# The pool mixer in another order: rows times weights first, then means less the row as products with a constant band matrix

## What is computed

```python
POOL_WINDOWS = (2, 4, 8, 16)          # one for each group of 256 channels

def pool_mixer(h, w_pool, b_pool, ls):
    ...
    for g, w in enumerate(POOL_WINDOWS):
        xg = hf[..., g * POOL_CH:(g + 1) * POOL_CH]
        cs = jnp.concatenate([jnp.zeros_like(xg[:, :1]), jnp.cumsum(xg, axis=1)], axis=1)
        lo = jnp.clip(t - w // 2, 0, n)
        hi = jnp.clip(t + w // 2, 0, n)
        mean = (cs[:, hi] - cs[:, lo]) / (hi - lo).astype(jnp.float32)[:, None]
        outs.append(mean - xg)
    p = jnp.stack(outs, axis=2).astype(h.dtype)
    y = jnp.einsum('bngc,gcd->bngd', p, w_pool) + b_pool
    return y.reshape(h.shape) * ls

def modulate(x, g, shift, scale):
    return rmsnorm(x, g) * (1.0 + scale) + shift
...
    x = x + g1 * y_lat                              # y_lat = pool_mixer(a_lat, ...), the same for the context
    x = x + g2 * hier_moe(modulate(x, norm2_g[i], sh2, sc2), ...)
```

## Time and profile before

| | before |
|---|---|
| median of 3 runs | 2318.79 us (2317.77 to 2321.14) |
| profiled execution | 2315.83 us, its span 2314.4 us |
| TensorE busy | 2145.6 us (93% of the span) |
| DVE, ACT, POOL busy | 1326.8, 1033.6, 155.3 us |
| granted TensorE clock, mean | 0.963 of full speed |

### The profile page before, as it was taken

How to read it: one execution, slowest core, us unless ns; L and a number is a source line. 1 busy time by engine, 2 the same in 40 slices (tenths; PEclk the granted TensorE clock), 3 DMA queues, 4 the chain that set the end, 5 groups by cost and what they waited for, 6 DMA issues and landing times.

```text
span 2314.4 us, 31372 instructions
## 1 busy us (share of the span) xinstructions
PE 2145.6 (93%) x13228; PEld 1644.9 (71%) x13228; DVE 1326.8 (57%) x1866; ACT 1033.6 (45%) x1499; POOL 155.3 (7%) x128
## 2 busy tenths in 40 slices
PE   4879989999996998999889999998999998999997
PEld 3556655577775675777667888886777776888885
DVE  4767766666637775355536766435254545766633
ACT  3446642155625664387744433324233354433321
POOL 0312200000001220000010000003000002000000
PEclk8989999999997998999999999999999999999998
DMA  9689980022217995211012222222222112322210
GB/s 397 282 317 369 380 346 0 0 110 111 80 48 286 350 359 195 109 37 37 37 73 109 109 75 108 109 91 68 78 88 94 47 40 84 122 83 109 107 58 37
DMA packets 39613, 320.67 MB, mean 139 GB/s; under 512 B 7167, under 2 KB 8191, under 8 KB 20735
## 3 DMA queue, kind: packets, MB, share of 16 engines
q1 hardware_dynamic: 26328, 285.44, 31.9%
q0 software_dynamic: 10624, 25.71, 3.3%
q10 hardware_dynamic: 2512, 7.41, 0.8%
HBM read 306.93 MB, written 24.19 MB: 143 GB/s over the span
## 4 chain that ended last, share of the span: by engine, by line
PE 83%; DVE 7%; ACT 4%; DMA 3%; issue 1%; SPq 1%; POOL 0%; ACTq 0%; POOLq 0%; DVEq 0%
PE PS L163 78%; PE PS L815 2%; PE PS L565 1%; DMA ring<-in_wmod 1%; DVE work L2230 1%; DMA work<-tokens,slots 1%; ACT work L1499 1%; PE PS L1076 1%; DVE WR L2236 1%; DVE work L1741 1%; ACT work L1504 0%; ACT L1504 0%; DMA tokens<-work 0%; ACT work L1495 0%; DVE XH L1728 0%
## 5 line engine op out<-in xcount | busy, mean ns | idle before, releaser
L163 PE MATMUL PS<-HS,RS 128*128 128x512 f32 x4128 | 953.4, 392 | 11.2 <-DVE HS L2007 8.6
L163 PEld LDWEIGHTS PS<-HS,RS 128*128 128x128 f32 x4128 | 775.6, 189 | 177.8 <-issue 14.0
L1685 DVE TENSOR_TENSOR RS<-ring,RS 128x1024 fp32r<-128x1024 f32 x212 | 258.8, 1224 | 344.7 <-ACT RS L1186 344.7
L1186 ACT ACTIVATE RS<-ring 128x1024 fp32r<-128x1024 f32 x212 | 221.4, 1051 | 255.3 <-PE PS L163 255.3
L1596 ACT ACTIVATE work<-work,vec 128x512 f32<-128x512 f32 x88 | 71.8, 816 | 239.8 <-DVE work L2354 239.8
L1685 DVE TENSOR_TENSOR CR<-ring,WR 128x1024 fp32r<-128x1024 f32 x128 | 153.3, 1221 | 39.3 <-ACT WR L1186 36.8
L1186 ACT ACTIVATE WR<-ring 128x1024 fp32r<-128x1024 f32 x128 | 134.8, 1058 | 55.1 <-PE PS L163 46.6
L163 PE MATMUL PS<-work 128*64 128x128 f32 (+5 forms) x1696 | 142.6, 305 | 8.3 <-DVE work L2293 4.4
L1186 ACT ACTIVATE work<-PS 128x384 f32<-128x384 f32 (+2 forms) x194 | 86.8, 484 | 130.0 <-PE PS L1076 45.8
L163 PEld LDWEIGHTS PS<-work 128*64 128x64 f32 (+2 forms) x1696 | 107.7, 148 | 37.9 <-issue 21.3
L163 PE MATMUL PS<-RS,HS 128*128 128x512 f32 x480 | 116.3, 401 | 8.2 <-DVE HS L2007 8.2
(11 more groups left out here) (250 smaller groups left out, 2842.4 us busy)
## 6 DMA issues: line engine op xcount, KB each, us to landing
ring<-in_wexp SPq DMA_DIRECT2D x32, 2048.0 KB, 11.0
ring<-in_wmod SPq DMA_DIRECT2D x24, 2048.0 KB, 10.4
ring<-in_ffnu SPq DMA_DIRECT2D x22, 2048.0 KB, 8.1
ring<-in_wexp SPq DMA_DIRECT2D x32, 1024.0 KB, 11.2
ring<-in_ffnd SPq DMA_DIRECT2D x10, 2048.0 KB, 7.2
ring<-in_dilqk SPq DMA_DIRECT2D x6, 2048.0 KB, 8.1
ring<-in_sbqk SPq DMA_DIRECT2D x4, 2048.0 KB, 8.1
ring<-in_dilv SPq DMA_DIRECT2D x3, 2048.0 KB, 8.1
```

Source lines behind the costliest of these rows:

```text
L163: return T.matmul(out, l, r, start=start, stop=stop, skip_group_check=True)
L1186: return S.activation(out, x, ACT.Copy, **kw)
L1685: V.tensor_tensor(lo, src, hi.bitcast(F32), ALU.subtract).then_inc(w_lo, 1)
```

## The change

The linear map and the mean along the tokens commute, so the order is turned round. First PE multiplies the scaled and shifted rows with the mixer's weights (`z`), tokens on partitions: a tile of 128 tokens is the stationary operand, the weights move, and one `z` is 128 tokens by 512 channels. ACT and DVE copy it out of PSUM in turns. Then `means` multiplies, for each chunk of 128 channels, the tiles of `zt` with a constant band matrix, `band`, which holds mean less row, 144 columns a tile, with two narrow pieces of 8 columns for the ends of a stream. DVE multiplies by the gate and adds to `XL` and `XC` in one instruction; the bias has been added there by POOL before. The sliding sums, their zeros and their patches go, and so does ACT's step behind the products. The constant comes in with the mixer's weights (2688 columns in place of 2048); the table for the stream ends goes (64 columns).

The latent stream is done first, then the context. ada 8, 9 and 10 stand behind the spreads of the second norm, ada 11 inside `route` behind the logits, and the row products of 14 and 15 behind the first three slot products (`info`). Some semaphores are renamed, and three memsets at the start become one.

```diff
         def pool_mix():
-            for n in (4, 5):
-                ada(n, 6 + n % 2)
-            pe.wait_ge(ld_work, 16)
-            pe.wait_ge(md_a, 16)
-            for g in range(4):
-                pe.wait_ge(pw_win, g + 1)
-                for mo in range(2):
-                    for s, (o, L) in enumerate(((0, 512), (512, 256))):
-                        i = 4 * g + 2 * mo + s
-                        pe.wait_ge(pl_y, i - 3)
-                        for k in range(2):
-                            x = mm(PS[:, 2 + i % 4, 0:L], poolw[:, g, k, mo * 128:(mo + 1) * 128],
-                                   PT[:, 2 * g + k, o:o + L], k == 0, k == 1)
-                        x.then_inc(pl_mm, 1)
...
+            def z(i):
+                t, hf = z_of(i)
+                pe.wait_ge(ld_work, 16)
+                free("z", i)
+                for g in (2 * hf, 2 * hf + 1):
+                    pe.wait_ge(md_b, 8 * (t // 4) + 2 * g + 2)
+                    for k in range(2):
+                        x = mm(PS[:, bank["z", i], g % 2 * 256:g % 2 * 256 + 256], HT[:, 2 * g + k, t * 128:(t + 1) * 128],
+                               poolw[:, g, k, :], k == 0, k == 1)
+                x.then_inc(pl_z, 1)
...
+                for j, t in enumerate(tiles):
+                    for q in (n for n in range(12) if z_of(n) == (t, c // 4)):
+                        pe.wait_ge(*z_copied(q))
+                    zc = zt[:, t, c * 128:(c + 1) * 128]
+                    if j == 0:
+                        mm(out[:, 0:8], zc, B[:, 144:152], True, False)
+                    a, b = (16 if j == 0 else 0), (128 if j + 1 == len(tiles) else 144)
+                    x = mm(out[:, 128 * j - 8 + a:128 * j - 8 + b], zc, B[:, a:b], False, False)
+                    if j + 1 == len(tiles):
+                        x = mm(out[:, 128 * j + 120:128 * j + 128], zc, B[:, 152:160], False, True)
+                x.then_inc(pl_mm, 1)
...
+            for i in range(4):
+                z(i)
+            ada_cols(4, 6)
+            for i in range(4, 8):
+                z(i)
+            pe.wait_ge(ad_mod, 4)
+            ada_rows(5, 7)
+            ada_cols(5, 7)
+            for c in range(8):
+                means(c)
+                if c > 2:
+                    stat_add(2, c - 3)
+                if c == 4:
+                    pe.wait_ge(ad_mod, 5)
+                    ada_rows(6, 6)
+            for i in range(8, 12):
+                z(i)
...
+            pe.wait_ge(pl_x, 16)
+            stat_spread(2)
+            stat_spread(3)
+            for n in (8, 9, 10):
                 ada(n, 6 + n % 2)
...
             pe.wait_ge(md_a, MD[1 + 2 * layer] + 8 * len(segs))
+            if layer == 0:
+                ada(11, 7)
...
+            scaled(0, 0, (0,), lambda c, s: HT[:, c, 0:512], 2)
+            for i in (0, 2, 4, 6):
+                z(i)
             ada(4, 6)
             ada(5, 7)
             pool_gates()
...
+            scaled(0, 0, (1,), lambda c, s: HT[:, c, 512:768], 2)
+            for i in range(8):
+                add(i)
+            z(8)
+            z(10)
+            ada(6, 6)
+            for i in range(8, 16):
+                add(i)
...
+        pool.wait_ge(ad_aff, 6)
+        for s, X in enumerate((XL, XC)):
+            pool.wait_ge(md_a, 8 * s + 8)
+            for c in range(8):
+                G.tensor_scalar(X[:, c, :], X[:, c, :], plv[:, 1, c, s:s + 1], None, ALU.add).then_inc(pl_b, 1)
...
-        Y.dma_start(W(12000, 2048), A["poolw"]).then_inc(ld_work, 16)
+        Y.dma_start(W(12000, 2688), A["poolw"]).then_inc(ld_work, 16)
```

More of the change, by code:

```diff
@@ L178, in build @@
     md_a, md_b = sem("mod_scaled"), sem("mod_shifted")
[L179 removed]
+    pl_z, pl_zd, pl_za, pl_mm, pl_b, pl_x = [sem("pool_" + n) for n in (
+        "z", "z_dve", "z_act", "means", "biased", "x")]
     rt_lg, rt_lt, rt_tr, rt_exp, rt_m, rt_rk, rt_blk = [sem("route_" + n) for n in ("logits", "biased", "turned", "exp", "chosen", "rank", "blocks")]
@@ new lines, in means @@
+            def means(i):
+                s, c = i // 8, i % 8
+                tiles = (range(4), range(4, 6))[s]
+                B, out = band[:, c // 2, :], PS[:, bank["b", i], :]
+                free("b", i)
+                for j, t in enumerate(tiles):
[9 more added lines that the diff above has]
+                x.then_inc(pl_mm, 1)
@@ L543, in route @@
                 rank_products()
-            else:
+            for e in range(3):
+                info(layer, nt, e)
+            if layer == 0:
                 pe.wait_ge(th_c, 12)
@@ L1224, in pool_mix, with rows, z @@
         def pool_mix():
+            def rows(s):
+                for c in range(8):
+                    h = HT[:, c, 0:512] if s == 0 else HT[:, c, 512:768]
+                    act.wait_ge(md_a, 8 * s + c + 1)
+                    S.activation(h, h, ACT.Identity, bias=mod[:, 0, c, s:s + 1]).then_inc(md_b, 1)
+            def z(i):
+                t, hf = z_of(i)
+                act.wait_ge(pl_z, i + 1)
+                copy(zt[:, t, hf * 512:hf * 512 + 512], PS[:, (4, 5, 2)[JOBS.index(("z", i)) % 3], :]).then_inc(pl_za, 1)
             act.wait_ge(ad_aff, 2)
-            shifted(0, 0, (0, 1), lambda c, s: PH[:, c, 8:520] if s == 0 else PH[:, c, 536:792])
+            rows(0)
             ada(4, 6)
+            for i in (1, 3, 5, 7):
+                z(i)
             ada(5, 7)
[L1229 to L1236, removed]
-                        S.activation(W(9600 + (s * 2 + c % 2) * 512, L), PS[:, 2 + i % 4, 0:L], ACT.Identity,
-                                     scale=plv[:, 0, c, s:s + 1], bias=plv[:, 1, c, s:s + 1]).then_inc(pl_y, 1)
-                    if c:
-                        square(2, c - 1, XL[:, c - 1, :], pl_x, 2 * c - 1)
-                for n in range(2 * g + 6, min(2 * g + 8, 10)):
-                    ada(n, 6 + n % 2)
-            ada(10, 6)
-            table(0)
-            square(2, 7, XL[:, 7, :], pl_x, 15)
+            rows(1)
+            for c in range(8):
+                square(2, c, XL[:, c, :], pl_x, c + 1)
+            z(9)
+            z(11)
+            root(2)
+            ada(6, 6)
+            for c in range(8):
+                square(3, c, XC[:, c, :], pl_x, 8 + c + 1)
+            ada(7, 7)
+            root(3)
+            for n in (8, 9, 10):
+                ada(n, 6 + n % 2)
         def route(layer, nt):
             HD = A["tokens"]
+            if layer == 0:
+                ada(11, 7)
             S.activation(tiny[:, 2:3], C("eps"), ACT.Exp)
@@ L1641, in act_program @@
         pool_mix()
-        root(2)
-        root(3)
-        ada(11, 7)
         act.wait_ge(ad_aff, 8)
@@ L2682, in _constants @@
     put("one16", 1.0)
-    e = np.zeros((4, 16), f)
-    for g in range(4):
-        h = 1 << g
-        for t in range(h):
-            e[g, t] = f(1.0) / f(t + h)
-        for k in range(h - 1):
-            e[g, 8 + k] = f(1.0) / f(2 * h - 1 - k)
-    put("edge", e.reshape(1, 64))
     put("eps", EPS)
```

167 lines of the change are left out of this document (77 added, 90 removed).

## The result

Over four executions each, side by side, the changed kernel took 2330.19 us (2329.12 to 2334.49) and the kernel before 2318.28 (2316.34 to 2321.14): ratio 1.0054, 95% interval 1.0036 to 1.0071. It is slower by 12 us, 0.5%. The profiled execution took 2330.0, its span is 2328.2, against 2314.4 of before. The forecast was 2330.4 for a profiled execution and 2333.4 for the median.

The account below looks back on a forecast made before the run. The chain up to the last token store's landing at 139.2 was taken to bound the kernel. Program order 7.7 plus queueing 6.9 gave +14.6: 2315.8 to 2330.4 profiled, median 2333.4 with 3.0 added; range 2322 to 2340.

Parts of the forecast that it names:

- The rival without queueing (1): Last token stores: loads don't hold them up, only program order counts; +7.7 us, 2326.5; chance 0.15.
- the hidden loads (2): Mixer on TensorE: edge weight loads and hand-overs are hidden; +1.2 us, 2320.0; chance 0.09.
- POOL as pace (3): Mixer: POOL's bias additions set the pace, deciding above 1.6 us each; +23 us, 2341.8; chance 0.07.
- Start, +0.8: Opening: the mixer's weight load grows from 1024 to 1344 KB on the chain, +0.8 us; three memsets go, 0.3.
- z, 1.78: Mixer on TensorE: one z is 4 products of 256 columns, 1.78 us; eight make 14.2.
- Means, 1.37 and 0.87: Mixer on TensorE: us per latent and context chunk, including 0.43 and 0.43 for narrow products at 0.107 a load.
- The cheap edges: Narrow products at only a floor of about 25 ns: a chunk 0.33 us cheaper, result +9.3 instead of +14.6.
- Steps with square sums, 1.62 and 1.02: Mixer on TensorE: a mean plus its square sum, adding 0.25 us in five latent steps, 0.15 in five context steps.
- POOL, 1.28 a bias, 0 as lower bound: Mixer: each POOL bias addition priced at 1.28 us; eight from 66.5 end at 76.8, ahead of TensorE's pace.
- Routing: Scaling starts at 108.8, logits end at 119.7; copies and DVE's expert choice 7.7 us late, last store issued at 136.6.
- Queueing: DMA: four loads and six token tiles, 29.7 us of work, done at 152.6, landed at 153.8; 6.9 us of delay.
- From the profile to the median, +3.0: Whole kernel: median of three runs taken as 3.0 us above the profiled time, 2330.4 to 2333.4.

Follow-up runs that it names:

- Experiment 1: Kernel before with ada 11 alone moved behind the logits, as in the changed kernel, sliding sums kept: 2326.13 us, ratio 1.0031.
- experiment 2: Changed kernel with the row products of ada 11 moved back ahead of the routing's scaling: 2325.19 us, ratio 1.0043 to the kernel before.
- experiment 3: Kernel before with the load of the second expert's up weights issued only after that expert's rows were gathered: 2319.37 us, ratio 1.0008.
- experiment 5: Changed kernel without the 8-column products, their columns given to the neighbours (stream ends wrong): 2330.5 us, ratio 1.0056 to the kernel before.
- experiment 6: Changed kernel with POOL adding the bias to only 64 columns of each chunk: 2331.39 us, one execution.
- experiment 7: Kernel before with the load of the mixer's weights (1024 KB) moved behind modulation piece 4: 2315.45 us, ratio 0.9982.
- the combined version: Changed kernel with end-tile tables replacing narrow products, mixer loads later, ada 11's rows early, bias added within ACT's square: 2320.99 us, ratio 1.0001 to before.
- experiment 9: Changed kernel with end-tile tables replacing narrow products, mixer loads behind pieces 4 and 5, ada 11's rows early: 2320.56 us, ratio 1.0013 to before.
- experiment 4: Changed kernel with the load of the second expert's up weights issued only after that expert's rows were gathered: 2328.9 us, ratio 1.0048 to before.

## Why the prediction was right, and where it was off

**The mechanism was the one forecast:** program order moves the last store, and the loads of pieces 14 and 15, let go by the late ada 11, make it land slower. Forecast 7.7 and 6.9; in the profiles 7.6 (136.55 less 128.91) and 7.4 (17.63 less 10.25). Experiment 1 has the second term without the new mixer, 7.1. That the sum of the profiles fits within 0.4 us (14.2 in place of 14.6) is partly luck. Its terms miss by up to 1.6 us and offset one another, and the mixer of the profile that it starts from is 3.2 us quicker than in the two other profiles of the same mixer with the load in the same place. The measured change of the medians is 11.9 us. The rival without queueing (1) is out by experiments 1, 2 and 3, the hidden loads (2) by experiment 5, POOL as pace (3) by experiment 6.

**Terms of the sum.**
- *Start, +0.8:* partly seen. The row products of piece 4 begin at 44.54 against 44.28 in the earlier trace rows, and the first z at 47.94, not 48.5; DVE's first scaling starts at 43.52, not 44.2. Over all profiles with the load in that place, five of the new mixer (44.54 to 44.84) and three of the old (43.95 to 44.28), the row products are 0.5 us apart. The load's bytes do count there, as experiment 7 shows from the other side (1024 KB gone, -3.0 us), more than the 2.4 that 431 GB/s makes of them.
- *z, 1.78:* 7.17 and 7.07 for four, right.
- *Means, 1.37 and 0.87:* 1.40 and 0.93, right within 0.06; a record of a narrow product, 0.107 from the nearest row, is 0.098 in experiment 5. The cheap edges, which would have made it +9.3, are out with that.
- *Steps with square sums, 1.62 and 1.02:* mis-sized, measured 1.83 and 1.33 from start to start. A step is more than its two parts: 1.40 for the means and 0.29 for eight records of sums (24 in a row take 0.86) make 1.69, and in experiment 5 1.01 + 0.29 = 1.30 stand against a step of 1.51. For the context 0.93 + 0.14 = 1.07 stand against 1.33, in experiment 5 0.53 + 0.14 = 0.67 against 1.00. So 0.14 us goes in each of the five latent steps and 0.26 in each of the five context steps where the two kinds alternate (0.21 and 0.33 in experiment 5). It is the largest part of why the routing's scaling starts at 110.4 and not 108.8.
- *POOL, 1.28 a bias, 0 as lower bound:* 1.55, above my price, 0.05 below the point from which I said it decides. DVE waited for POOL three times (0.41, 1.20, 0.37 us). TensorE, which runs ahead of it by three banks, didn't.
- *Routing:* logits end at 120.3 (forecast 119.7), the store goes out at 136.55 (136.6). Of the 1.6 us by which the scaling was later than forecast, 0.3 came back in ACT's shifts (8.19 against 8.46), 0.7 in the tail of the logits behind them, and the rest between the first and the last store.
- *Queueing:* landed at 154.2, forecast 153.8.
- *The rest:* forecast unchanged, it is 1.2 us shorter in the profile (2173.1 against 2174.3), within chance.
- *From the profile to the median, +3.0:* this is the step that missed. I took the 3.0 us by which before's profiled execution lay below the median of its three runs for a property of the kernel. The changed kernel's profiled execution (2330.0) is 0.2 below its median. The profile of before was a quick one; the 3.2 us of its mixer (experiments 1 and 3) are of the right size for it, though how often the mixer runs that way no run counts. A sum made against it should have been read as a difference between two executions, each with its own few us of chance.

**Not settled:** no run moved ada 8, 9 and 10 back ahead of the spreads, so that the late modulation loads cost the combined version its 4.0 us is read from the traces and not shown by an experiment. Its first expert load goes out later as well (118.5 against 116.6 us). Nor did a run try the steps without alternation, to price that by itself. And what the new mixer alone costs in time, with every load and every ada in the old order, was not measured.

## What to carry to other kernels

When a change takes work from a busy engine, look first at whether that engine's work was what ended last and then at which transfers the new order lets go, and when: here one modulation step had moved behind the logits, and with it two loads out of a stretch with room into the busiest 30 us. By itself that step is worth some 8 us at the first gather in the old kernel and 6 in the new one, of 15.0, and 4 to 7 us of the 12 in time (experiments 1 and 9; the 2.5 of experiment 2 are within chance). A store of small rows beside loads of large ones got its share by packets, not by bytes (120 packets of 0.43 MB beside 121 of 1.72), so it was done only when nearly everything was. Before a sum is laid on one profile, a second profile of the same kernel tells how much of it is chance: here 3.2 us in the very stretch that was changed. Holding back a load that is needed next only shifted the wait (experiments 3 and 4). What paid was moving one earlier, or taking one off the start that nobody waits for yet (experiment 7).

## What was new about the hardware

- The packets' fair share: 121 packets of the load queue with 1.72 MB beside 120 of the token queue with 0.43 MB in 5 us. The Trainium skill (DMA: Bandwidth & Descriptors, Queues, rings and completion order) says that an engine takes turns between queues by packets; the trace agrees, and adds what it costs: a 512 KB store landed after 3.3 us when no load was in its way and after 17.6 in such company.
- GpSimd's one-input addition with a value for each partition took 1.55 us for 128 x 512 fp32 (0.90 for 256 columns, 0.42 for 64), slower than its two-input addition of the same size at 1.28. The eight in a row took the same time, 1.55 to 1.57, however busy DVE was beside them. The Trainium skill (GPSIMD Engine Reference, Engine selection) has one-input work there at "roughly line-rate", which would put it ahead of the two-input one; here the measurement decides.
- Steps that alternate between full products and products in 32-column strips took TensorE 0.14 to 0.33 us more than the same records of either kind in a row (1.83 against 1.69, 1.33 against 1.07). That the alternation itself is the reason is argued, not shown.
- An fp32 product of 8 columns cost two records of 0.098 us each here, near the 0.106 of a weight load in the earlier trace rows, and nothing of it was hidden.
